# Two pairs of column chunks of a token projection by seven half-size products each, in a float32 kernel on one core

## What is computed

```python
def _mixer(h, positions, w_in, forget_bias, w_branch_a, w_branch_b, w_out):
    proj = h @ w_in
    ...
    q_a, k_a, v_a, q_i, k_i, w_i, q_f, k_f, v_f, f_f, gates = jnp.split(proj, offs, axis=-1)
    q_a = _partial_rope(q_a.reshape(B, S, H_SPARSE, HEAD_DIM), positions, ROT_DIM)
```

## Time and profile before

| | us |
|---|---|
| median of three runs | 3422.16 |
| the profiled execution | 3422.93 |
| its span on the engines | 3421.2 |
| PE busy | 3339.3 (98%) |
| ACT busy | 1430.8 (42%) |
| POOL busy | 1485.0 (43%) |
| DVE busy | 1784.3 (52%) |
| first token projection | 1834.3 to 1954.1 |
| second token projection | 2622.9 to 2742.6 |

### The profile page before, as it was taken

How to read it: one execution, slowest core, us unless ns; L and a number is a source line. 1 busy time by engine, 2 the same in 40 slices (tenths; PEclk the granted TensorE clock), 3 DMA queues, 4 the chain that set the end, 5 groups by cost and what they waited for, 6 DMA issues and landing times. The chain is left out here.

```text
span 3421.2 us, 48805 instructions
## 1 busy us (share of the span) xinstructions
PE 3339.3 (98%) x19319; PEld 2751.0 (80%) x19319; DVE 1784.3 (52%) x3104; ACT 1430.8 (42%) x2870; POOL 1485.0 (43%) x1337
## 2 busy tenths in 40 slices
PE   8999999999999999999999999999999999999999
PEld 7768778888877688888888877888888877888887
DVE  4665574636457674665363286445154176545243
ACT  4562354323344554532323236344343245444343
POOL 3330154454443545444544443444554443445543
PEclk9999999999999999999999999999999999999999
DMA  3210024544221022345443220222323220123321
GB/s 113 83 50 10 27 87 136 194 150 164 98 98 50 26 93 92 107 140 185 154 154 100 96 74 14 74 87 93 104 85 102 84 86 27 50 86 99 99 93 56
DMA packets 232830, 317.83 MB, mean 93 GB/s; under 512 B 9909, under 2 KB 149148, under 8 KB 232604
## 3 DMA queue, kind: packets, MB, share of 16 engines
q1 hardware_dynamic: 203206, 261.55, 23.6%
q10 hardware_dynamic: 29398, 53.17, 4.6%
HBM read 312.59 MB, written 2.10 MB: 92 GB/s over the span
## 5 line engine op out<-in xcount | busy, mean ns | idle before, releaser
L366 PE MATMUL banks<-split,split 128*128 128x512 f32 (+2 forms) x11760 | 2683.0, 389 | 22.5 <-ACT split L385 13.7
L366 PEld LDWEIGHTS banks<-split,split 128*128 128x128 f32 x11760 | 2185.9, 188 | 496.1 <-ACT split L385 24.5
L389 POOL TENSOR_TENSOR split<-kept,split 128x512 fp32r<-128x512 f32 (+2 forms) x1158 | 1356.1, 1175 | 1622.8 <-ACT split L385 1619.9
L385 ACT ACTIVATE split<-kept 128x512 fp32r<-128x512 f32 (+2 forms) x1158 | 646.1, 564 | 1454.8 <-PE banks L366 1411.4
L1916 DVE SCALAR_TENSOR_TENSOR work<-banks,kept,work 128x511 f32<-128x511 f32 (+1 forms) x176 | 120.4, 746 | 257.0 <-ACT work L1898 256.2
L913 DVE SCALAR_TENSOR_TENSOR work<-work,kept 128x512 f32<-128x512 f32 x168 | 195.5, 1164 | 6.0
L858 DVE SCALAR_TENSOR_TENSOR kept<-banks,kept 128x512 f32<-128x512 f32 x48 | 33.3, 746 | 209.6 <-PE banks L366 209.6
L856 DVE TENSOR_TENSOR kept<-banks,kept 128x512 f32<-128x512 f32 x64 | 40.6, 685 | 195.0 <-PE banks L366 195.0
L543 DVE COPY work<-banks 128x512 f32<-128x512 f32 (+1 forms) x64 | 37.4, 644 | 195.1 <-PE banks L366 195.0
L1855 DVE TENSOR_TENSOR work<-work,banks 128x512 f32<-128x512 f32 x44 | 28.3, 685 | 165.7 <-ACT work L1843 165.7
L1542 ACT ACTIVATE work<-work 128x128 f32<-128x128 f32 (+3 forms) x160 | 89.5, 560 | 49.9 <-DVE work L1602 49.1
(11 more groups left out here) (445 smaller groups left out, 3179.6 us busy)
## 6 DMA issues: line engine op xcount, KB each, us to landing
work<-in_mod_w ACTq DMA_DIRECT2D x48, 1024.0 KB, 6.2
kept<-in_ffn_w SPq DMA_DIRECT2D x94, 512.0 KB, 4.8
kept<-in_w_up SPq DMA_DIRECT2D x88, 512.0 KB, 4.6
kept<-in_w_in SPq DMA_DIRECT2D x36, 1024.0 KB, 5.0
kept<-in_od_w_in SPq DMA_DIRECT2D x20, 1024.0 KB, 5.1
kept<-in_ffn_w SPq DMA_DIRECT2D x18, 1024.0 KB, 5.2
kept<-in_w_down SPq DMA_DIRECT2D x18, 1024.0 KB, 5.0
kept<-in_ev_w_in SPq DMA_DIRECT2D x8, 1024.0 KB, 5.3
```

Source lines behind the costliest of these rows:

```text
L366: m = pe.matmul(self.bank(q, j), lhs, rhs, start=t == 0 and i == 0, stop=t == job.KT - 1 and i == 2)
L385: act.activation(self.weights(s, 0), self.source(s), ACT.Copy).then_inc(self.rounded, 1)
L389: pool.tensor_tensor(self.weights(s, 1), self.source(s), self.weights(s, 0), ALU.subtract).then_inc(self.k.slices_split, 1)
```

## The change

The token job becomes a `QuadJob` of four chunks. Chunk 0 is columns 1024 to 1536, chunk 1 the last 208 columns; both are computed as before. Chunks 2 and 3 are pairs of 512-column chunks: columns 0 to 1024, and 1536 to 2560. For a pair, the activations A (512 x 1024) and the weights B (1024 x 1024) are cut into quarters and the product is made by Winograd's form of Strassen's method: seven products of 256 x 512 by 512 x 512, of which each is four slices of 2 token tiles x 3 = 6 matmuls. A pair is thus 28 slices (`steps`), where two chunks were 16 slices of 12 matmuls.

Four combinations of the quarters of A (`make_sums`, then rounded by ACT and split by DVE in `sum_rest`) are made once and serve both pairs. Four combinations of the quarters of B are made for each pair by DVE in place, in the ring, slice by slice (`combine`, 16 operations of 128 x 512): T3 before product P7, T2 before P6, T4 before P4, T1 before P5. ACT waits for each before it rounds the slice. A slot of the ring is loaded again only when its last combination has been made too (`LAST_MADE`). The products are added into `T` by ACT (2 copies) and DVE (`add`, 14 sums of a bank and a tile of `T`).

```diff
+class QuadJob(Job):
+    HALF = 4
+    P1, P2, P3, P7, P6, P4, P5 = range(7)
+    ROWS_COLS = ((0, 0), (HALF, 0), (HALF, 512), (0, 512))
+    UNIT_OF = (0, 1, 2, 3, 0, 1, 2)
+    LAST_SPLIT = (20, 24, 28, 16)
+    LAST_MADE = (16, 12, 16, 8)
...
+    def steps(self, c):
+        return 7 * self.HALF if c in self.pair_cols else self.KT
...
+                        unit_end[u.slot] = [(self.slices_split, slices + w.LAST_SPLIT[i]),
+                                            (self.combined, 16 * pairs + w.LAST_MADE[i])]
...
     def round_slice(self, act, s):
-        if t == u.t0:
+        if c in job.pair_cols:
+            p, i = t // job.HALF, t % job.HALF
+            if p in job.MADE_AT:
+                act.wait_ge(self.k.combined, job.paired[c][2] + job.MADE_AT[p] + i + 1)
+            elif i == 0:
+                act.wait_ge(self.k.units_loaded[u.slot], u.loaded)
...
+class TakeQuads(Finish):
...
+    def ready_bank(self, pe, c, p):
+        job, n = self.job, 14 * self.pair(c)
...
+        elif p == job.P6:
+            pe.wait_ge(self.copied, 2 * self.pair(c) + 2)
+        elif p == job.P4:
+            pe.wait_ge(self.added, n + self.D11)
+        elif p == job.P5:
+            pe.wait_ge(self.added, n + self.U2)
...
+    def pair_scalar(self, act, s, q, c, t):
+        if self.pair(c) == 0 and t in self.ROUND_AT:
+            m = self.ROUND_AT[t]
+            act.wait_ge(self.sums, 8)
+            act.activation(self.sum_hi[:, m, :], self.sum_at(m), ACT.Copy).then_inc(self.sums_rounded, 1)
+        if t == job.HALF - 1:
+            self.await_product(act, s, t, job.P1)
...
+            for j in range(2):
+                act.activation(self.col(c, 0, 2 + j), self.bank(c, job.P1, j), ACT.Copy).then_inc(self.copied, 1)
...
+    def combine(self, dve, c, what, i):
...
+        elif what == job.T2_AT:
+            dve.wait_ge(k.combined, made + job.T3_AT + i + 1)
+            dve.wait_ge(k.slices_split, split + job.P1 * job.HALF + i + 1)
+            out, a, b, op = b11, b12, b11, ALU.add
...
+        dve.tensor_tensor(at(out), at(a), at(b), op).then_inc(k.combined, 1)
...
+    def pair_vector(self, dve, link, s, q, c, t, pending):
...
+        if t == 0 and first:
+            for m in (self.S4, self.S3, self.S2, self.S1):
+                self.sum_rest(dve, m)
+        elif t == 1:
+            for i in range(4):
+                self.combine(dve, c, job.T3_AT, i)
+        elif t == 5:
+            for i in range(4):
+                self.combine(dve, c, job.T2_AT, i)
+        elif t == 9:
+            for i in range(4):
+                self.combine(dve, c, job.T4_AT, i)
+            self.await_product(dve, s, t, job.P2)
...
+            self.add(dve, c, job.P2, c11, c21, 0)
+        elif t == 11:
+            self.combine(dve, c, job.T1_AT, 0)
+            self.combine(dve, c, job.T1_AT, 1)
+        elif t == 19:
+            self.await_product(dve, s, t, job.P6)
+            self.add(dve, c, job.P6, c21, c21, self.D11)
+            self.combine(dve, c, job.T1_AT, 2)
+            self.combine(dve, c, job.T1_AT, 3)
+            self.add(dve, c, job.P7, c22, c21, self.U2)
+            self.add(dve, c, job.P3, c12, c21, 0)
+        elif t == 23:
+            self.await_product(dve, s, t, job.P4)
+            self.add(dve, c, job.P4, c21, c22, self.D12)
+        elif t == 27:
+            self.await_product(dve, s, t, job.P5)
+            self.add(dve, c, job.P5, c22, c22, self.C21)
+            self.add(dve, c, job.P5, c12, c12, self.D12)
+            if first:
+                for d in (0, 1):
+                    pending.append(self.side.rotate_done(dve, link, d, self.added, 14))
...
-    plan[f"tok{l}"] = Job(d["w_in_2"][l], [512] * 5 + [N_TOK - 2560], tokens=ST)
+    plan[f"tok{l}"] = QuadJob(d["w_in_2"][l], ((1024, 512), (2560, N_TOK - 2560)), (0, 1536), ST)
```

More of the change, by code:

```diff
@@ L91, in __init__, with total, tiles, steps @@
             self.parts = parts
+    pair_cols, paired = {}, {}
     def tiles(self, c):
         return self.tokens or -(-self.widths[c] // P)
+    def steps(self, c):
+        return self.KT
+    def total(self):
+        return sum(self.steps(c) for c in range(len(self.widths)))
+class QuadJob(Job):
[5 more added lines that the diff above has]
+    LAST_MADE = (16, 12, 16, 8)
+    T3_AT, T2_AT, T4_AT, T1_AT = 0, 4, 8, 12
+    MADE_AT = {P7: T3_AT, P6: T2_AT, P4: T4_AT, P5: T1_AT}
+    def __init__(self, W, plain, pairs, tokens):
+        super().__init__(W, [plain[0][1], plain[1][1], 512, 512], tokens=tokens, parts=[
+            [(0, *plain[0])], [(0, *plain[1])], [(0, pairs[0], 512)], [(0, pairs[1], 512)]])
+        assert self.KT == 2 * self.HALF
+        self.pair_cols = {2: pairs[0], 3: pairs[1]}
+        self.paired = {}
+    def tiles(self, c):
+        return 1 if c in self.pair_cols else self.tokens
+    def steps(self, c):
+        return 7 * self.HALF if c in self.pair_cols else self.KT
 class Unit:
@@ L182, in plan_weights @@
     def plan_weights(self, plan):
-        slices, loaded, self.units = 0, [0] * UNITS, []
+        slices, pairs, loaded, self.units = 0, 0, [0] * UNITS, []
         unit_end = [[] for _ in range(UNITS)]
@@ L189, in plan_weights @@
             for c, width in enumerate(w.widths):
+                if c in w.pair_cols:
+                    quarters = []
+                    for i, (t0, col) in enumerate(w.ROWS_COLS):
+                        u = Unit(w, c, t0, w.HALF, len(self.units) % UNITS)
+                        u.parts = [(0, w.pair_cols[c] + col, 512)]
+                        loaded[u.slot] += 16
+                        u.loaded, u.after = loaded[u.slot], unit_end[u.slot]
+                        unit_end[u.slot] = [(self.slices_split, slices + w.LAST_SPLIT[i]),
+                                            (self.combined, 16 * pairs + w.LAST_MADE[i])]
+                        quarters.append(u)
+                        self.units.append(u)
+                    for t in range(w.steps(c)):
+                        w.unit_of[c, t] = quarters[w.UNIT_OF[t // w.HALF]]
+                    w.paired[c] = (quarters, slices, 16 * pairs)
+                    slices += w.steps(c)
+                    pairs += 1
+                    continue
                 most = min(w.KT, UNIT // width)
@@ L305, in __init__ @@
                 tiles += job.tiles(c)
-                for t in range(job.KT):
+                for t in range(job.steps(c)):
                     self.slices.append((q, job, c, t, finish, hi, lo))
@@ L310, in __init__ @@
             assert job.slice0 == first
-            first += len(job.widths) * job.KT
+            first += job.total()
             finish.of(self, job)
@@ L340, in source @@
         u = job.unit_of[c, t]
-        return self.k.unit_view(u)[:, t - u.t0, :]
+        return self.k.unit_view(u)[:, t % job.HALF if c in job.pair_cols else t - u.t0, :]
     def tensor(self, pe):
@@ L390, in rest_of_slice, with walk @@
             self.k.slices_split, 1)
-    def walk(self, ahead, side, rate, beside=iter(())):
+    def walk(self, ahead, side, rate, beside=iter(()), pair=None):
         pending = []
@@ L412, in walk @@
                 ahead(s + SLOTS)
-            if t == job.KT - 1:
+            if job.pair_cols:
+                pair(finish, s, q, c, t, pending)
+            if c not in job.pair_cols and t == job.KT - 1:
                 pending.append(side(finish, q, c))
@@ L430, in scalar @@
         self.walk(lambda s: self.round_slice(act, s), lambda f, q, c: f.scalar(act, q, c), lambda f: f.rate,
-                  self.beside.scalar(act, None, None) if self.beside else iter(()))
+                  self.beside.scalar(act, None, None) if self.beside else iter(()),
+                  lambda f, s, q, c, t, pending: f.pair_scalar(act, s, q, c, t))
     def vector(self, dve):
@@ L435, in vector @@
         self.walk(lambda s: None, lambda f, q, c: f.vector(dve, link, q, c), lambda f: f.rate,
-                  self.beside.vector(dve, link, None, None) if self.beside else iter(()))
+                  self.beside.vector(dve, link, None, None) if self.beside else iter(()),
+                  lambda f, s, q, c, t, pending: f.pair_vector(dve, link, s, q, c, t, pending))
     def run(self):
@@ L4493, in tokens_job @@
     T = k.view(A_WORK + DT * S, ST, N_TOK)
-    take = Take(lambda c, j: T[:, j, c * 512:min((c + 1) * 512, N_TOK)], after=rms, flush=0,
-                side=Rotated(k, T, SCRATCH_AT))
-    return plan[f"tok{l}"], take, rms.hi, rms.lo
+    sums_at = A_WORK + DT * S + ST * N_TOK
+    take = TakeQuads(k, T, lambda first, width, j: T[:, j, first:first + width], rms, sums_at,
+                     Rotated(k, T, sums_at + 8192))
+    job = plan[f"tok{l}"]
+    return job, take, rms.hi, rms.lo
 def second(k, plan, l, out):
```

158 lines of the change are left out of this document (153 added, 5 removed).

## The result

The changed kernel takes 3437.36 us (median of 6 runs, 3436.39 to 3438.99) against 3421.07 us for the kernel before (6 runs): a ratio of 1.0045, 95% interval 1.0035 to 1.0055, so 16.3 us slower. Its profiled execution took 3438.99 us, 16.1 more than that of before. PE does fewer matmuls (19223 for 19319) and its busy time stays as it was, in a span that is 16.1 us longer.

The account below looks back on a forecast made before the run. PE bounded the kernel before; in the changed pairs, POOL and DVE taking turns would. Per layer 95.6 - 87.0 + 1.8 = 10.4 us slower, 20.8 for both: 3443.7, given as 3442.5 us; range 3418 to 3462.

Parts of the forecast that it names:

- POOL and DVE in turns of 1.71 us: In the pairs, a split and a DVE operation with two SBUF sources alternate, 1.71 us a turn, against PE's 1.36.
- The first pair: Each layer's first two chunks: P4 starts at 33.7 us, the pair ends at 44.6, 38.1 without waits.
- ACT's wide roundings: First pair's start: four 1024-element roundings at 1.05 us each, bounds 0.63 and 2 x 0.63, before the last sum_rest.
- The two copies behind them: First pair, behind the last sum_rest: two copies on DVE at 0.684 us each, done at 11.8 us.
- the chain of twelve combinations: First pair, before P4: twelve combinations on DVE in turns with POOL, 20.5 us, then two sums, 1.4.
- The second pair: Each layer's last two chunks: starts at 47.3 us after a late weight load, 2.7 lost, and ends at 95.6.
- T2's wait: Second pair: T2 stands behind rotations and T3 on DVE; its first two operations are done at 73.4 us.
- The stage's end: After the last product of a layer's token job: four sums of 0.685 us, 2.7 in all, so 1.8 more.
- The sum: Whole kernel: 10.4 us a layer slower, 20.8 for both; 3443.7 from the profiled execution, given as 3442.5.
- The clock: Rival of a lower clock in PE's waits: it stays at 1.00 where PE waits for POOL; no chance of its own.
- The shared path alone: Rival for the pairs: DVE's order costs nothing more; 88 us, 2.8 a layer more with the end, 3428; chance 0.12.
- Turns of whole instructions: Rival for the pairs: split and combination exclude each other entirely; 1.97 us a turn, 6.2 a layer more, 3455; chance 0.05.

Follow-up runs that it names:

- spread: Changed kernel with DVE's work reordered: sum_rest one every second slice, combine one a slice from the fifth to the twentieth, rotations late; 3436.65 us, ratio 1.0046.
- split_on_dve: Against spread, DVE instead of POOL makes the splits of the pairs' slices; 3411.70 us, ratio 0.9973 to the kernel before.
- rotate_late: Changed kernel with only the eighteen rotation operations a layer moved, to the second pair's last third; 3437.91 us, ratio 1.0050 to the kernel before.

## Why the prediction was right

The direction, the mechanism and the size held; 3442.5 was forecast, 5 above the median. In some places terms that missed cancelled, and these were luck.

- **What bounds it.** POOL and DVE in turns of 1.71 us: measured 1.71. Each side taken away by itself brought the pairs to between 76 and 81 us, and moving the splits from POOL to DVE alone, from spread to split_on_dve, from 89 to 80, so this is shown, not only argued.
- **The first pair.** P4 was to start 33.7 us after P1 and did at 33.2; ACT's wide roundings, taken at 1.05 from narrower ones, took 1.048; the pair was to end at 44.6 and ended at 45.2. Two terms on the way missed and cancelled. The four `sum_rest` hardly waited for those roundings (0.23 us, before the first) but followed each other on DVE, 8.17 us for the four, and the last ended at 11.5, not 10.4. The two copies behind them are of 208 columns and took 0.64 together, where the sum had 0.684 each. And the chain of twelve combinations, which the forecast takes as what holds P4 back, adds little to POOL's own turns: PE's wait before P4 is 0.63 us, and in spread, which has no such block, P4 starts at 32.5.
- **The second pair.** Its first weights were to land at 45.7 and did at 45.3. T2's wait came at 72.2, forecast for about 74; P4 at 82.5, for 84.7, in both layers: three of the last ten rotation operations were caught behind a split where four were counted, and three combinations T2 ran free where two were. The pairs' end at 95.6 was met by 95.3 in the first layer and 93.6 in the second. The first is luck: P4 and P5 took 12.8 us there, for 10.9 in the sum and 11.2 in the second layer, beside a stretch at a granted clock of 0.50 (below), and this hides that P4 was 2.2 us early.
- **The stage's end.** 1.8 us forecast, 1.6 measured (2.84 less 1.25).
- **The sum.** 20.8 us forecast, 16.1 measured between the profiled executions. The terms that missed are the second layer's end of the pairs (2.0 us) and what no term stood for: what follows each token job became 0.8 and 1.5 us shorter, against 0.7 us more ahead of the first.
- **The clock**, which I gave no chance of its own, took part. The prediction reads it as full throughout, but a digit of the earlier trace rows stands for a 40th of the span, and the trace behind it has stretches of 3.4 and 6.8 us at 0.50 (below). By the traces it nearly cancels: some 1.6 us more in the first layer's pairs, and 0.7 us more, 0.8 and 1.5 us less in the code that is the same. The low stretch from 1941.0 should cost nothing, since PE waits 1.99 us for DVE before P4 behind it. This is read from the traces and was not tried by itself; the profiled execution of the changed kernel, with a mean clock of 0.993, is the slowest of its six, and the other five have 0.994 or 0.995.
- **The rivals.** The shared path alone, at 88 us a layer, was the right size for the pairs in the order that spreads the work (spread, 89), but not a time that the kernel could have: the rotations had to stand somewhere. Turns of whole instructions, the rule of the Trainium skill (SBUF — State Buffer, section Who interferes with whom), would be 1.97 us; the trace has 1.71 here too. Even by the steps at which each engine alone follows itself, 1.256 for a split and 0.60 for a combination (four in 2.49 us, the last 0.69 long), it would be 1.86 us. On who contends it is borne out: the sums with a source in PSUM kept 0.68 us, those with two sources in SBUF took 1.56.

The expectations that failed were behind the prediction: that the order is worth 12 us (rotate_late) or 10 (spread). It holds in part for the pairs (4 to 6 us a layer) and not for the kernel, since the same operations then stand before the end of the stage.

## What to carry to other kernels

Before work moves to an engine that looks half idle, count how often its new operations will meet those of the engine that shares its path to SBUF, and price both at the turn that some row of the trace already shows, not at their lengths alone. Here a saving of 10.9 us of matmuls a layer halved the time of a slice for PE alone and left the split of each slice as long as it was: a product cut to half size needs its weights prepared twice as fast. And an operation taken off the path inside a stage may stand before its end; read both places before it counts as gained.

## What the runs showed of the hardware that was not expected

One engine doing all was faster than two sharing, once the order was mended too: 28 splits and 16 combinations a pair took POOL and DVE some 1.6 us each when shared, and DVE alone 0.69 (3410.3 and 3411.7 us, for 3436.7 with the splits on POOL in the same order as the second).

The granted clock fell from 1.00 to 0.50, the 1.2 GHz level, within the second pair of the changed kernel, after PE had been idle for 1.73 us (and 0.94 soon after), and again after 1.99 us. Busy times by stretch of the first layer (the third column from the right is the granted clock), and the start of the next stage:

```profile
1941.00:1944.40 3.40, 2.94 (x7) 2.36 (x8) 3.40 (x3) 1.26 (x2) 3.40 (x3) 0.50 0.00 0
...
1951.30:1954.60 3.30, 3.30 (x9) 2.54 (x8) 3.30 (x5) 0.63 (x1) 3.19 (x2) 0.50 0.01 2
...
1964.90:1971.70 6.80, 6.00 (x17) 5.06 (x18) 5.01 (x11) 5.21 (x8) 4.98 (x4) 0.50 0.53 196
```

The kernel before had its low stretches elsewhere, among them these, some 90 and 114 us behind the first token job:

```profile
2045.20:2048.40 3.20, 3.20 (x9) 2.49 (x8) 3.13 (x10) 0.42 (x1) 0.73 (x1) 0.50 0.00 0
2069.10:2072.30 3.20, 3.20 (x14) 2.35 (x13) 1.37 (x5) 2.60 (x10) 1.13 (x2) 0.50 0.00 0
```

In the changed kernel the same places, 10.7 us later, have a clock of 1.00, and the stretch between the two token jobs is 0.8 us shorter. The second layer has a low stretch in its pairs once, not twice, and they are 1.6 us shorter there, all of it behind the start of P4, where the first layer has its second low stretch. That these differences are the clock's was not tried by itself. Why a low stretch is missing where one stood before is left open.
